# Second part of the modulation summed by VectorE in column pieces, and four low quarters moved to GpSimd

## What is computed

```python
mod = (jax.nn.silu(c) @ w_mod[l] + b_mod[l])          # c: 1 x 1024, w_mod: 1024 x 6144
sh1, sc1, g1, sh2, sc2, g2 = jnp.split(mod, 6, axis=-1)
h = _modulate(_rms_norm(x, norm1_g[l]), sh1, sc1)
q_a, k_a, v_a, q_b, k_b, v_b = _in_proj(h, w_in[l])    # w_in: 1024 x 2304, 1024 + 256 tokens
...
x_new = x + g1 * _merge(o_a, o_b, on_a[l], on_b[l], w_out[l])
h2 = _modulate(_rms_norm(x_new, norm2_g[l]), sh2, sc2)
x_new = x_new + g2 * _swiglu(h2, w_gate[l], w_up[l], w_down[l])
```

## Time and profile before

| | |
|---|---|
| median of 3 runs | 2321.15 us (2320.94 to 2322.6) |
| the profiled execution, its own time | 2320.64 us |
| its span, first to last instruction | 2318.9 us |
| TensorE busy in the span | 2263.4 us, 98% |
| VectorE busy | 1481.0 us, 64% |
| ScalarE busy | 1020.7 us, 44% |
| GpSimd busy | 365.6 us, 16% |
| mean granted clock of TensorE | 0.995 of 2.4 GHz |

### The profile page before, as it was taken

How to read it: one execution, slowest core, us unless ns; L and a number is a source line. 1 busy time by engine, 2 the same in 40 slices (tenths; PEclk the granted TensorE clock), 3 DMA queues, 4 the chain that set the end, 5 groups by cost and what they waited for, 6 DMA issues and landing times. The chain is left out here.

```text
span 2318.9 us, 34643 instructions
## 1 busy us (share of the span) xinstructions
PE 2263.4 (98%) x12884; PEld 1867.7 (81%) x12884; DVE 1481.0 (64%) x2408; ACT 1020.7 (44%) x2030; POOL 365.6 (16%) x342
## 2 busy tenths in 40 slices
PE   6999999999999999999999999999989999999998
PEld 3878778878878888888888976988878888888886
DVE  3533278776687777776689423234587777666687
ACT  3523178875343232323444433233355555444444
POOL 2493400154340000000001000131240000000011
PEclk9999999999999999999999999999999999999999
DMA  8142350015213232326654411113224444666553
GB/s 321 37 147 90 120 120 28 2 47 167 107 58 124 89 126 86 119 87 214 212 186 142 148 37 46 38 38 143 103 96 150 150 152 148 239 202 217 173 168 123
DMA packets 156129, 289.73 MB, mean 125 GB/s; under 512 B 11998, under 2 KB 59820, under 8 KB 152764
## 3 DMA queue, kind: packets, MB, share of 16 engines
q1 hardware_dynamic: 155964, 287.52, 36.8%
HBM read 219.04 MB, written 70.62 MB: 125 GB/s over the span
## 5 line engine op out<-in xcount | busy, mean ns | idle before, releaser
L2270 PE MATMUL ps<-ff_b_hi,ff_a_hi 128*128 128x512 f32 x448 | 174.5, 390 | 0.2 <-DVE ff_b_lo L2258 0.2
L2271 PE MATMUL ps<-ff_b_lo,ff_a_hi 128*128 128x512 f32 x448 | 174.3, 389 | 0.0
L2272 PE MATMUL ps<-ff_b_hi,ff_a_lo 128*128 128x512 f32 x448 | 174.3, 389 | 0.0
L2231 ACT ACTIVATE ff_a_hi<-ff_a_raw 128x512 fp32r<-128x512 f32 x112 | 70.7, 631 | 157.3 <-PE ps L2272 149.9
L1964 ACT ACTIVATE swiglu_w_hi<-swiglu_stage 128x512 fp32r<-128x512 f32 x110 | 69.0, 630 | 160.6 <-PE ps L2023 151.9
L2021 PE MATMUL ps<-ht_hi,swiglu_w_hi 128*128 128x512 f32 x352 | 137.8, 392 | 0.6 <-DVE ht_lo L1916 0.6
L2022 PE MATMUL ps<-ht_lo,swiglu_w_hi 128*128 128x512 f32 x352 | 137.0, 389 | 0.0
L2023 PE MATMUL ps<-ht_hi,swiglu_w_lo 128*128 128x512 f32 x352 | 137.0, 389 | 0.0
L2256 DVE TENSOR_TENSOR ff_a_lo<-ff_a_raw,ff_a_hi 128x512 fp32r<-128x512 f32 x112 | 80.6, 719 | 83.2 <-ACT ff_a_hi L2231 83.2
L453 DVE TENSOR_TENSOR w_lo<-stage,w_hi 128x2048 fp32r<-128x2048 f32 x23 | 58.9, 2562 | 112.6 <-ACT w_hi L449 112.4
L2270 PE MATMUL ps<-swiglu_b_hi,swiglu_a_hi 128*128 128x512 f32 x308 | 120.3, 391 | 0.4 <-DVE swiglu_b_lo L2258 0.4
(11 more groups left out here) (466 smaller groups left out, 6479.9 us busy)
## 6 DMA issues: line engine op xcount, KB each, us to landing
ff_a_raw<-ff_act_dram SPq DMA_DIRECT2D x112, 256.0 KB, 2.7
swiglu_a_raw<-swiglu_act_dram SPq DMA_DIRECT2D x77, 256.0 KB, 2.8
stage<-w_in SPq DMA_DIRECT2D x18, 1024.0 KB, 5.2
stage<-w_mod SPq DMA_DIRECT2D x16, 1024.0 KB, 4.6
ff_stage<-w_ff SPq DMA_DIRECT2D x16, 1024.0 KB, 5.4
ff_act_dram<-ff_act_sums SPq DMA_DIRECT2D x16, 1024.0 KB, 4.3
ff_act_dram<-ff_acts SPq DMA_DIRECT2D x16, 768.0 KB, 5.6
swiglu_stage<-w_gate SPq DMA_DIRECT2D x11, 1024.0 KB, 6.3
```

The source lines that it names most:

```text
L2231: act.activation(a_hi[r][:, :], a_raw[s % LOOK][:, :], ACT.Copy).then_inc(f.a2_hi, 1)
L2270: pe.matmul(bank, a_hi[r][:, cols], b_hi[r][:, :], start=first, stop=False)
L2271: pe.matmul(bank, a_hi[r][:, cols], b_lo[r][:, :], start=False, stop=False)
L2272: return pe.matmul(bank, a_lo[r][:, cols], b_hi[r][:, :], start=False, stop=last)
```

## The change

TensorE's 16 groups of products are taken out. Instead each of the 4096 columns is summed by VectorE over the eight row sets: for 16 blocks of 256 columns, eight instructions of 128x256 each (`modx_dve`, one instruction a "piece" below, eight pieces one "sum", sums numbered 0 to 15). Each piece but the first of a sum takes the running total from SBUF, and waits by a semaphore for the piece before. After every four sums TensorE adds the 128 partitions by four products of 256 columns (`modx_pe`), at four places. The weights come as 32 transfers of 512 KB, two to a sum, into two halves of a buffer; each waits until the half has been used up by VectorE (`modx_step`). VectorE's sums are written between its other work in `dve_x`. The split of load 7 stands later on both engines, after narrow tile 6. In the attention, the four low quarters go to GpSimd, behind the rows; three of the rows come after the last table; the third and fourth high quarter come one unit later or, the third, at the next pair's first.

```diff
+        def mod_half_of(x):
+            m = x // 2
+            first = 2 * D * (1 + m // 8) + 512 * (m % 4) + 256 * (m % 8 // 4)
+            return t["w_mod"][0].rearrange("(p k) n -> p k n", k=KT)[:, 4 * (x % 2):4 * (x % 2) + 4, first:first + 256]
...
-                else:
-                    sp.wait_ge(modx_part, m)
-                sp.dma_start(stage[:, :], mod_rows_of(m)).then_inc(mod2_landed, 16)
+                for x in (2 * m, 2 * m + 1):
+                    if x >= 2:
+                        sp.wait_ge(modx_step, 4 * (x - 1))
+                    sp.dma_start(mod_raw[:, x % 2, :, :], mod_half_of(x)).then_inc(mod2_landed[x % 2], 16)
...
             for j in range(NT):
                 if j == 4:
                     heads_scale(dve, 0)
+                    modx_dve(dve, 0)
                     split_lo(dve, 4, 0)
+                    modx_dve(dve, 1)
                 wide_sum(dve, 1, j)
             split_lo(dve, 5, 1)
+            modx_dve(dve, 2)
+            modx_dve(dve, 3)
             for j in X_TILES[2]:
                 if j == 4:
+                    modx_dve(dve, 4)
+                    modx_dve(dve, 5)
                     heads_scale(dve, 1)
                 if j == NT:
+                    modx_dve(dve, 6)
+                    modx_dve(dve, 7)
                     split_lo(dve, 6, 0)
                 wide_sum(dve, 2, j)
             modx_dve_rows(dve, 0)
-            split_lo(dve, 7, 1)
             for j in range(N_TILES):
                 narrow_sum(dve, j)
+                if j in (1, 3):
+                    modx_dve(dve, 8 + j // 2)
+                if j == 6:
+                    split_lo(dve, 7, 1)
             split_lo(dve, 8, 0)
             heads_scale(dve, 2)
+            for m in range(10, 13):
+                modx_dve(dve, m)
             heads_scale(dve, 3)
+            for m in range(13, 16):
+                modx_dve(dve, m)
             modx_dve_rows(dve, 1)
...
+            for k in range(KT):
+                if k % 4 == 0:
+                    dve.wait_ge(mod2_landed[k // 4], 16 * (m + 1))
+                piece = mod_raw[:, k // 4, k % 4, :]
+                if k == 0:
+                    dve.tensor_scalar(total[:, :], piece, cond[:, 0, k:k + 1], None, ALU.mult).then_inc(modx_step, 1)
+                else:
+                    dve.wait_ge(modx_step, KT * m + k)
+                    dve.scalar_tensor_tensor(out=total[:, :], in0=piece, scalar=cond[:, 0, k:k + 1], in1=total[:, :],
+                                             op0=ALU.mult, op1=ALU.add).then_inc(modx_step, 1)
+
+        def modx_pe(pe, q):
+            pe.wait_ge(modx_step, 4 * KT * (q + 1))
+            h, u = q // 2, q % 2
             for g in range(4):
-                mm = pe.matmul(ps[32 * g:32 * g + 2, 4 + h, :], cond[:, :, k], stage[:, 512 * g:512 * (g + 1)], start=(k == 0), stop=(k == KT - 1))
-            mm.then_inc(modx_part, 1)
+                mm = pe.matmul(ps[32 * g:32 * g + 2, 4 + h, 256 * u:256 * u + 256], neg_half[:, 0:2], mod_sum[g][:, :], start=True, stop=True)
+            mm.then_inc(modx_made, 1)
...
                 if i == PAIRS - 1:
-                    rows_a(pool)
+                    roots_a(pool)
+                    rows_a(pool, range(5))
                 for j in range(2):
                     table_inner(pool, i, j)
+            rows_a(pool, range(5, NT))
+            for q in range(4):
+                quarter_low(pool, q)
...
-            for n in wide_pe(pe, 1):
-                if n in (8, 11, 14):
-                    modx_pe_part(pe, (n - 8) // 3, n == 8)
             for n in wide_pe(pe, 2):
-                if n % 3 == 1:
-                    modx_pe_part(pe, 3 + n // 3, False)
+                if n == 5:
+                    modx_pe(pe, 0)
+                if n == 19:
+                    modx_pe(pe, 1)
             narrow_pe(pe)
             for n in wide_pe(pe, 3):
-                if n in (4, 6, 9, 11, 14, 16):
-                    modx_pe_part(pe, 10 + (4, 6, 9, 11, 14, 16).index(n), False)
+                if n in (7, 17):
+                    modx_pe(pe, 2 + n // 17)
```

More of the change, by code:

```diff
@@ L91, in program @@
     rstd = fixed("rstd", [16])
-    junk = at("junk", [D], mybir.dt.bfloat16, region(2 * D))
+    junk_at = region(2 * D)
+    junk = at("junk", [D], mybir.dt.bfloat16, junk_at)
     hsum = fixed("hsum", [10, 8])
@@ L117, in program @@
     mod_row = at("mod_row", [512], F32, xnr + 6144)
+    mod_raw = at("mod_raw", [2, 4, 256], F32, ring)
+    mod_sum = [at(f"mod_sum{g}", [256], F32, x) for g, x in enumerate((xnr + 4096, xnr + 5120, junk_at, junk_at + 1024))]
     mod_part = at("mod_part", [512], F32, xnr)
@@ L199, in program @@
         laid_out, bias_in = early("laid_out"), early("bias_in")
-        mod2_landed, modx_part, modx_row, modx_stored = (early(x) for x in ("mod2_landed", "modx_part", "modx_row", "modx_stored"))
+        modx_step, modx_made, modx_row, modx_stored = (early(x) for x in ("modx_step", "modx_made", "modx_row", "modx_stored"))
+        mod2_landed = [early(f"mod2_landed{b}") for b in range(2)]
         ka_tr, ka_hi, ka_lo = early("ka_tr"), early("ka_hi"), early("ka_lo")
@@ L262, in staged @@
             return stage_2 if p in SECOND else stage
-        def mod_rows_of(m):
-            first = 2 * D * (1 + m // KT)
-            return t["w_mod"][0].rearrange("(p k) n -> p k n", k=KT)[:, m % KT, first:first + 2 * D]
+        def mod_half_of(x):
+            m = x // 2
+            first = 2 * D * (1 + m // 8) + 512 * (m % 4) + 256 * (m % 8 // 4)
+            return t["w_mod"][0].rearrange("(p k) n -> p k n", k=KT)[:, 4 * (x % 2):4 * (x % 2) + 4, first:first + 256]
         def mod_bias(sp, h):
@@ L284, in mod_piece @@
                     sp.wait_ge(w_lo_done, P_X + 1)
-                elif m == 10:
+                if m == 10:
                     sp.wait_ge(w_lo_done, P_X + 9)
-                else:
-                    sp.wait_ge(modx_part, m)
-                sp.dma_start(stage[:, :], mod_rows_of(m)).then_inc(mod2_landed, 16)
+                for x in (2 * m, 2 * m + 1):
+                    if x >= 2:
+                        sp.wait_ge(modx_step, 4 * (x - 1))
+                    sp.dma_start(mod_raw[:, x % 2, :, :], mod_half_of(x)).then_inc(mod2_landed[x % 2], 16)
             mod_piece(0)
@@ L304, in sync_x @@
                 mod_piece(m)
-            sp.wait_ge(modx_part, 10)
+            sp.wait_ge(modx_step, 80)
             sp.dma_start(in_piece(stage), x_piece(3, 0)).then_inc(w_landed, 16)
@@ L648, in act_x @@
                 wide_evict(act, 2, j)
-            split_hi(act, 7, 1)
             for j in range(N_TILES):
                 narrow_evict(act, j)
+                if j == 6:
+                    split_hi(act, 7, 1)
             split_hi(act, 8, 0)
@@ L787, in program, with modx_dve @@
         ROPED = 6 * 2 * 3
[L790 to L794, removed]
+        def modx_dve(dve, m):
+            total = mod_sum[m % 4]
+            if m == 0:
+                dve.wait_ge(tl_done, T_O)
+            if m >= 4:
+                dve.wait_ge(modx_made, m // 4)
+            for k in range(KT):
[11 more added lines that the diff above has]
+            h, u = q // 2, q % 2
             for g in range(4):
-                mm = pe.matmul(ps[32 * g:32 * g + 2, 4 + h, :], cond[:, :, k], stage[:, 512 * g:512 * (g + 1)], start=(k == 0), stop=(k == KT - 1))
-            mm.then_inc(modx_part, 1)
+                mm = pe.matmul(ps[32 * g:32 * g + 2, 4 + h, 256 * u:256 * u + 256], neg_half[:, 0:2], mod_sum[g][:, :], start=True, stop=True)
+            mm.then_inc(modx_made, 1)
         def modx_dve_rows(dve, h):
-            dve.wait_ge(modx_part, KT * (h + 1))
+            dve.wait_ge(modx_made, 2 * (h + 1))
             dve.wait_ge(modb_in, 64 * (h + 1))
@@ L803, in modx_dve_rows @@
                 one = slice(32 * g, 32 * g + 1)
-                dve.tensor_tensor(mod_row[one, :], ps[one, 4 + h, :], mod_row[one, :], ALU.add).then_inc(modx_row, 1)
+                dve.scalar_tensor_tensor(out=mod_row[one, :], in0=ps[one, 4 + h, :], scalar=-2.0, in1=mod_row[one, :],
+                                         op0=ALU.mult, op1=ALU.add).then_inc(modx_row, 1)
         KA_BANK = (7, 4, 5)
@@ L1207, in act_o @@
             act.activation(o_t[:, :], ps[:, 7, 0:P], ACT.Copy).then_inc(ot_evac, 1)
-        QUARTER_AT = [unit(B, 2, 3), unit(B, 2, 5), unit(B, 2, 7), unit(B, 3, 0)]
+        QUARTER_AT = [unit(B, 2, 3), unit(B, 2, 5), unit(B, 3, 0), unit(B, 3, 1)]
         def attention_act(act):
@@ L1295, in attention_dve @@
                 dve_sides(dve, u)
-                if u in QUARTER_AT:
-                    quarter_dve(dve, QUARTER_AT.index(u))
         def table_edge(pool, i, j):
@@ L1392, in quarter_act, with quarter_low @@
             done_hi.then_inc(w_hi_done if q == 3 else quarter_hi, 1)
-        def quarter_dve(dve, q):
+        def quarter_low(pool, q):
             if q == 3:
-                dve.wait_ge(w_hi_done, P_O + 1)
```

(11 more changed lines are left out.)

## The result

The change made the kernel slower: median 2349.33 us (2346.45 to 2350.06, 4 runs) against 2321.64 (2320.94 to 2322.6, 4 runs), ratio 1.0108, 95% interval 1.0095 to 1.0121 (the two medians by themselves give 1.0119). The profiled execution took 2349.58 us, its span is 2348.0, 29.1 more than before.

What follows compares the result with a forecast made beforehand. TensorE was taken as the bound, VectorE having room and GpSimd none. -16.6 + 14.2 + 0.7 + 8.8 + 4.5 + 1.3 + 9.8 - 3.3 + 3.6 = +23.0 gave 2344 us; own range 2332 to 2356, overall 2321 to 2357.

Steps and rivals of the forecast that it cites:

- Taken off TensorE, -16.6: 16 old groups at 1.20 us removed (-19.2), four new half-width groups at 0.65 added (+2.6), without new waits.
- A piece, 0.51 behind the one before: On VectorE, a dependent piece follows its predecessor after 0.51 us; a sum takes 4.1 us, 65 us for 16.
- Alternation with GpSimd: Where GpSimd has a full queue, every VectorE piece waits out one whole GpSimd instruction.
- place 1: Start of panel 2: sum 1 ends at about 150, squares sums come late, TensorE waits for a bank: +14.2 us.
- place 2 with load 5: Panel 2, sums 2 and 3: load 5 ready late, +0.7 us; TensorE waits for sums 0 to 3, +8.8 us.
- place 3: End of panel 2: sums 6 and 7 late, +2.7 us, then load 6's low split before the narrow panel, +1.8.
- place 4 with load 8: Panel 3: load 8 later, +1.3 us; GpSimd's long gain gets in behind sum 10's first piece, sum 11 late, +9.8.
- Clock, +3.6: After three long TensorE waits: the first's loss is taken up, the other two may each cost 1.8 us; bounds 0 and 7.
- Attention, -3.3: TensorE's four waits for VectorE behind a low quarter, 3.8 us in all, go; at least 2 come back.
- A: Rival: pieces slip between GpSimd's instructions, sums fall in VectorE's idle time, some 5 us of transfer waits remain; 2306 us, chance 0.13.
- B: Rival: the wait at panel 2's start stands, those for sums 2-3 and in panel 3 are avoided; 2324 us, chance 0.15.
- C: Rival: half transfers sharing DMA engines with weight loads land late at every sum, +8 to +14; 2355 to 2360 us, chance 0.09.

Runs made afterwards that it cites:

- two_columns: The kernel before with its 64 old products cut from 512 columns to two; transfers, waits and the 16 places stay: 2315.77 us, ratio 0.9980.
- total_in_psum: The change with each sum's running total in an unused PSUM bank, only the last piece writing to SBUF: 2317.88 us, ratio 0.9984 to the kernel before.
- change_tables_first: The change with the bias table's transfers ahead of the modulation rows' wait on SyncE's queue, totals still in SBUF: 2344.84 us, ratio 1.0097.
- scaling_later: The change with sums 10 and 11 written ahead of the scaling of panel 2's heads instead of behind it: 2348.17 us, ratio 1.0114.
- all_three: total_in_psum with bias-table transfers earlier, GpSimd's sums read earlier, load 6's split before sum 7, second new group and bias rows inside narrow panel: 2307.95 us.
- short_gains: The change with most of GpSimd's gain and rotation of panel 0's heads left out, both piece operands still in SBUF: 2326.36 us, ratio 1.0024.

## Why the prediction was right, and where it was not

The mechanism and the places were right, and the total stayed in the forecast's own range of 2332 to 2356. Some of that was luck: the waits came out 2.9 smaller, the clock and the attention 9.2 worse.

- **Taken off TensorE, -16.6.** Right: two_columns gives 0.84 + 0.35 a group, 1.20 forecast. A new group took 0.62 (198.63 to 200.84 in total_in_psum, less a wait of 1.59), 0.65 forecast.
- **A piece, 0.51 behind the one before.** 0.52 (three pieces take 1.53, four 2.05). The 0.41 that I had worked out from the Trainium skill (VectorE: DVE Perf Modes, section "The DRAIN you can't avoid") was not seen.
- **Alternation with GpSimd.** Right, and shown from both sides: with the total in PSUM, and with GpSimd's work cut. What was not shown ahead: piece 0, with one operand in SBUF, waits as well (4.69), while with its result in PSUM it took 0.48.
- **The places.** Forecast against measured: place 1 14.2, 13.5; place 2 with load 5 9.5, 7.8; place 3 4.5, 3.7; place 4 with load 8 11.1, 11.4. Together 39.3 against 36.4. A half transfer took 3.5 us by the median of its issues; I took 4.0, and the estimate of 3.2 from the Trainium skill (SBUF — State Buffer, section "The DMA setup-cost knee") was nearer.
- **Clock, +3.6, bounds 0 and 7.** Too small, and outside its bounds. The attention begins 27.7 later, input loads apart; 36.4 of waits less 16.6 are 19.8; the other 7.9 are what is left over, and only the clock's rows are there to explain it. The step that failed is "the other two may each cost 1.8": the mean clock is below 0.95 in six of the ten windows of 20 us from 140 to 340, not behind the long waits alone.
- **Attention, -3.3.** The term was too small (-4.9 alone, -4.6 in change_tables_first), and it was lost in the change to the hole, +6.2 us of attention, which no step foresaw. I had followed SyncE's queue up to the sums, but not to the transfers behind the last store. So the profiled execution lost 28.9 instead of 23.0: waits -2.9, clock +4.3, attention +4.9, inputs +0.75, -1.0 after the attention, together +6.0.
- **The rivals.** A is refuted by the 12.04 and 9.20; but total_in_psum, which is A made true, gave 2318 and not 2306. 9.5 us of waits are left in it instead of the 5 that I priced, one of them behind GpSimd's reading, and the hole. B fell with the 7.80 and 9.20. C fell: half transfers were faster than taken.

Open: what lowers the clock from 1400 to 1500 in ten of the twelve profiles, with TensorE busy throughout; and by what way the transfers of `v_b` stop TensorE.

## What to carry to other kernels

Idle time of VectorE was no room for pieces with two SBUF operands while GpSimd's queue was full of gains and rotations (13.05 us for seven instead of 3.70): either one operand goes to PSUM, or the work goes where GpSimd rests. Taking a wait away is worth what is late next, so price that too; here the next wait took a gain, or part of it, in scaling_later, two_columns and all_three. And when one queue runs late, follow it to its end: transfers that slide against the code can leave an engine idle at a place that no wait names.

## What was not expected of the hardware

- TensorE stood still for 4.57 to 4.76 us, with no releaser in the trace, while 256 KB transfers and one 16 KB packet of instructions shared the DMA engines; with those transfers 8 us earlier the idle time was gone, and with them 33 us later 0.47 was left.
- GpSimd's root of the means, 10.76 us long (from 166.26), did not hold up the pieces: three took 1.53 from 171.04, beside it, and in short_gains seven took 3.68 beside the same one (143.89; GpSimd's from 138.08, 10.57 long). So not every GpSimd instruction here held the pieces up, and its length did not decide it.
- The granted clock fell to 0.93 to 0.97 in windows where TensorE was busy all 50 us.
